# A streaming encoder step: where the turning of results stands among TensorE's products, and what the S5 kernel products wait for

## The chip, the cores and the metric

The kernel runs on one core of one Trainium2 chip. The metric is the device time of one launch in microseconds, the median of several runs. The engines of the core are called TensorE (PE in the rows, PEld its weight loads), VectorE (DVE), ScalarE (ACT), GpSimd (POOL) and SyncE (SP); each works through its own instructions in program order, and they are tied together by semaphores.

## What is computed

One inference step of a hybrid layer on 2048 prompt tokens and 8 x 16 sample tokens, model width 1024. The input is normed and multiplied by one wide matrix, and its columns are parted among three mixers:

```python
h = rms_norm(x, norm_g)
fq, fk, fv, fg, ff, su, sg, mq, mg = split_columns(h @ w_in)
fq = rms_norm(fq.reshape(B, T, N_FOX_HEADS, HEAD_DIM), fox_q_norm)
fk = rms_norm(fk.reshape(B, T, N_FOX_HEADS, HEAD_DIM), fox_k_norm)
...
fox_out = fox_attend(fq, fk, fv, logf).reshape(B, T, FOX_WIDTH) * jax.nn.silu(fg)
ssm_y, h_re, h_im = s5_mixer(su, h0_re, h0_im, a_re, a_im, log_dt, b_re, b_im, c_re, c_im, d, w_glu, b_glu)
ssm_out = ssm_y * jax.nn.silu(sg)
...
mix = jnp.concatenate([fox_out, ssm_out, mem_out], axis=-1) @ w_out
```

The change touches the first part alone, the projection `h @ w_in`, with what is computed of the S5 mixer (a diagonal state space of 16 groups) in between.

## The kernel before, in words

**Passes and visits.** The projection goes in seven passes over column groups: state (the forget logits, su and sg), keys, values, queries, memkv, memq, gate. Each pass visits 17 tiles of 128 tokens (memkv only the 2 tiles of the memory), 104 visits in all; visits 0 to 16 are the state pass, 17 to 33 the keys. A visit's product comes in three parts (`product`, L927 in the rows). The matrices are kept as a high and a low half, and the product is high x high, high x low and low x high: in parts 0 and 1 each x chunk's high half meets both halves of the weights, in part 2 the low halves of x meet the high weights. The first and the last visit of a pass go chunk by chunk instead, 3, 3 and 2 chunks to a part.

**The order.** `projection_order` writes one list of steps, and each engine's program walks through that same list and does its share of every step. After `product v, part` stand, in this order, loads of x for later visits, turnings of the input (`x`, state pass only), the next pass's weights in a pass's last visit, `first` (after part 0) and `second` (after part 1) for visit v-1, `split` (high and low halves of the next x, other passes), `turn` (after part 1, for visit v-2), and one slot of the work that is interleaved (the S5 steps, the decay, the sample's attention).

**Steps that matter here.**
- `x j`: TensorE turns input tile j (eight transposes, L882) into two banks; ScalarE first squares the input for the norm (L1193), then copies each bank twice, as high half xh (L1206) and as a whole xu (L1207); VectorE subtracts for the low half xl (L1515). Before `product v+1, 0` of the state pass comes `x` for visit v+1, placed after part 0 of visit v. In visits 7 and 12 the next item is a tile of the memory: it gets no product and only the copies xu, and the input of the next visit is then turned after part 1.
- `first v-1`, state pass: ScalarE takes the tanh of the gate (L1242, into th), VectorE scales su into `parts` (L1545), makes the logits (L1547), z (L1549), and the gate's half of `parts` (L1552).
- `turn v-2`: TensorE transposes the results of visit v-2 (L949; four of them, two for memkv and memq): `parts` in the state pass, which ScalarE copies in three instructions (L1263 twice, L1265); the normed heads, `stage`, in keys, queries, memkv and memq, of which ScalarE copies the high half (L1260) and VectorE subtracts the low half (L1595), and which SyncE then stores (L744). values and gate turn nothing.
- The banks of the state pass go in two pairs by the visit's parity, so product v+1 waits until th, su, logits and z of visit v-1 are read out.
- `s5_kern g`, g 0 to 7, in the keys pass: the pair g of the S5 kernel's impulse responses, kernels 2g and 2g+1, in three banks in rotation (kernel n in bank n mod 3), L993. Before pair g, TensorE waits until all 2g earlier kernels are copied (`s_kread`); VectorE copies each in `s5_kern_read` (L1603), one slot later, and waits for both products of the pair. Further S5 products are the drive products (L1008, read by L1615), which need the block matrix that SyncE's DMAs write, and the GLU products (L1054, followed by ScalarE's tanh L1295) in the queries pass.

## Time and profile before

| | us |
|---|---|
| median of 3 runs | 1411.63 |
| lowest, highest | 1405.93, 1411.88 |
| profiled execution, its own time | 1408.32 |
| its span, first to last instruction | 1406.4 |
| TensorE busy | 1369.0 |
| VectorE, ScalarE, GpSimd busy | 922.0, 636.6, 575.6 |

The mean granted clock of TensorE was 0.997 of full speed. The profile lists the busy time of each engine, the waits and what ended them, and the instructions in order of time. An engine's idle time counts only if the work that sets the end has to wait for it. A matmul's row runs from its start to a modelled end, so that rows of successive matmuls overlap; the distance between starts is what they cost.

### The profile page before, as it was taken

Reading aid. Unit: us, or ns where it says so; the run is one execution under the profiler, and the core shown is the slowest. Engines: PE = TensorE matmul, PEld = TensorE weight load, DVE = VectorE, ACT = ScalarE, POOL = GpSimd, SP = SyncE. Lnnn points to the kernel's source line nnn. Section 1 sums busy time; section 2 is a strip of 40 time slices with the busy share of each in tenths; the row PEclk is TensorE's granted clock in tenths of the full one; section 3 lists DMA queues with packets and bytes.
Section 4 is the critical chain, followed back from the end, with each engine's and each line's share of the span. In section 5 each row is a group of like instructions: output and inputs, shape, how many; then the busy total and the mean of one; then the engine's idle time right before and its main releaser. Section 6 shows DMA issues by size and latency. Waiting matters only on the chain.

```text
span 1406.4 us, 25060 instructions
## 1 busy us (share of the span) xinstructions
PE 1369.0 (97%) x8382; PEld 1086.1 (77%) x8382; DVE 922.0 (66%) x2025; ACT 636.6 (45%) x1364; POOL 575.6 (41%) x606
## 2 busy tenths in 40 slices
PE   8999999999999999999999999999999999999998
PEld 7999767788877777777777777777777777778886
DVE  3789755593376778666433676776776776497775
ACT  6766423332353354445333455555555655422121
POOL 2122442200033234221100556877977867644452
PEclk9999999999999999999999999999999999999999
DMA  7885699987349769787998767448458355556552
GB/s 234 295 281 199 201 268 252 275 273 228 113 139 272 248 223 266 243 266 237 313 321 264 170 189 158 107 98 181 103 109 181 83 114 196 160 169 199 191 177 89
DMA packets 211023, 284.21 MB, mean 202 GB/s; under 512 B 49809, under 2 KB 146481, under 8 KB 207409
## 3 DMA queue, kind: packets, MB, share of 16 engines
q1 hardware_dynamic: 209856, 282.61, 68.7%
q8 instruction: 69, 1.13, 0.3%
q14 instruction: 58, 0.47, 0.1%
q10 hardware_dynamic: 1040, 0.00, 0.0%
HBM read 191.12 MB, written 90.19 MB: 200 GB/s over the span
## 4 chain that ended last, share of the span: by engine, by line
PE 60%; DVE 3%; POOL 2%; ACT 2%; issue 2%; DMA 2%; SPq 1%; DVEq 0%; ACTq 0%; POOLq 0%
PE in_g L927 14%; PE attn_pv L2531 10%; PE attn_s L2601 6%; PE attn_s L2500 6%; PE attn_s L2505 5%; PE attn_pv L2601 5%; PE attn_s L2485 5%; PE attn_s L2513 2%; PE in_b L1102 1%; POOL in_hv L1810 1%; PE in_b L1054 1%; PE attn_s L2554 1%; PE attn_s L2502 1%; PE in_b L1157 1%; PE in_b L1122 1%
## 5 line engine op out<-in xcount | busy, mean ns | idle before, releaser
L927 PE MATMUL in_g<-in_wh,in_xh 128*128 128x512 f32 (+2 forms) x904 | 331.4, 380 | 6.2 <-ACT in_xh L1219 2.4
L927 PE MATMUL in_g<-in_wl,in_xh 128*128 128x512 f32 (+2 forms) x904 | 321.9, 369 | 0.0
L2807 POOL TENSOR_TENSOR attn_probs<-attn_probs,attn_probs_turned 128x512 f32<-128x512 f32 (+3 forms) x200 | 214.3, 1072 | 64.9 <-ACT attn_probs_turned L2633 40.9
L927 PE MATMUL in_g<-in_wh,in_xl 128*128 128x512 f32 (+2 forms) x904 | 236.4, 380 | 1.4 <-DVE in_xl L1532 1.3
L2847 DVE TENSOR_REDUCE attn_tops<-attn_s 128x1 f32<-128x512 f32 (+3 forms) x288 | 159.1, 596 | 108.6 <-PE attn_s L2485 108.6
L2633 ACT ACTIVATE attn_probs_turned<-attn_s 128x512 f32<-128x512 f32 (+1 forms) x352 | 161.2, 545 | 125.7 <-PE attn_s L2505 124.8
L927 PEld LDWEIGHTS in_g<-in_wh,in_xh 128*128 128x128 f32 x904 | 165.5, 189 | 40.8 <-issue 7.4
L927 PEld LDWEIGHTS in_g<-in_wl,in_xh 128*128 128x128 f32 x904 | 165.6, 189 | 27.9
L927 PEld LDWEIGHTS in_g<-in_wh,in_xl 128*128 128x128 f32 x904 | 159.1, 190 | 34.9 <-issue 5.3
L1808 POOL TENSOR_SCALAR in_hs<-in_hs 128x8 f32<-128x8 f32 (+1 forms) x53 | 19.5, 368 | 401.8 <-DVE in_hs L1559 401.8
L2531 PE MATMUL attn_pv<-attn_probs_turned,attn_v 128*64 128x256 f32 (+1 forms) x1216 | 142.1, 363 | 0.0
L1219 ACT ACTIVATE in_xh<-in_xu 128x512 fp32r<-128x512 f32 x174 | 99.6, 623 | 55.6 <-DMA in_xu<-scratch_xt 50.4
L2531 PEld LDWEIGHTS attn_pv<-attn_probs_turned,attn_v 128*64 128x64 f32 x1216 | 84.7, 136 | 41.2 <-issue 7.5
L1532 DVE TENSOR_TENSOR in_xl<-in_xu,in_xh 128x512 fp32r<-128x512 f32 x106 | 68.6, 688 | 35.7 <-ACT in_xh L1219 35.1
L1810 POOL TENSOR_TENSOR in_hv<-in_hs,all_neghalf 128x8 f32<-128x8 f32 (+1 forms) x53 | 85.4, 1611 | 4.4
L1260 ACT ACTIVATE in_x_turned<-in_tr 128x512 fp32r<-128x512 f32 (+1 forms) x53 | 27.6, 520 | 87.2 <-PE in_tr L949 78.9
L2805 POOL TENSOR_TENSOR attn_probs<-attn_probs_turned 128x512 f32<-128x512 f32 x40 | 52.7, 1327 | 30.4 <-ACT attn_probs_turned L2633 30.4
L2505 PE MATMUL attn_s<-all_x,all_y 100*128 100x512 f32 (+3 forms) x160 | 61.2, 382 | 1.6 <-ACT all_x L2622 1.6
L2500 PE MATMUL attn_s<-attn_qa,attn_ka 128*128 128x512 f32 (+3 forms) x160 | 62.1, 388 | 0.0
L2500 PE MATMUL attn_s<-all_x,all_y 128*128 128x512 f32 (+3 forms) x160 | 62.0, 388 | 0.0
L2505 PE MATMUL attn_s<-attn_qb,attn_kb 100*128 100x512 f32 (+3 forms) x160 | 61.2, 383 | 0.0
L1579 DVE TENSOR_TENSOR in_work<-in_g,in_hr 128x512 f32<-128x512 f32 (+1 forms) x53 | 31.4, 593 | 38.3 <-POOL in_hr L1813 37.2
(377 smaller groups left out, 2685.8 us busy)
## 6 DMA issues: line engine op xcount, KB each, us to landing
in_xu<-scratch_xt SPq DMA_DIRECT2D x87, 512.0 KB, 5.4
in_xl<-scratch_xt SPq DMA_DIRECT2D x34, 512.0 KB, 4.6
in_raw<-in_w_in SPq DMA_DIRECT2D x40, 256.0 KB, 5.2
scratch_xt<-in_xu SPq DMA_DIRECT2D x19, 512.0 KB, 4.4
scratch_xt<-in_xl SPq DMA_DIRECT2D x17, 512.0 KB, 5.0
scratch_k<-in_x_turned SPq DMA_DIRECT2D x17, 512.0 KB, 7.2
scratch_q<-in_x_turned SPq DMA_DIRECT2D x17, 512.0 KB, 5.4
in_x_turned<-in_x_prompt SPq DMA_DIRECT2D x16, 512.0 KB, 4.8
```

The lines of the kernel that those rows point to most:

```text
L927: last = X.matmul(g_ps[b][:, 0:m], x, ws[:, c, w0:w0 + m], start=(c == 0 and h == 0 and ws is wh), stop=(c == KC - 1 and h == 1))
L1219: F(xh[:, item_visit[j] % 2, 4 * h:4 * h + 4, :], xu[:, j % 2, 4 * h:4 * h + 4, :], ACT.Copy)\
L1532: V.tensor_tensor(xl[:, v % 3, 4 * h:4 * h + 4, :], xu[:, j % 2, 4 * h:4 * h + 4, :], fl(xh[:, v % 2, 4 * h:4 * h + 4, :]), ALU.subtract). ...
L1810: G.tensor_tensor(hv[:, 0:m], hs[:, 0:m], K.neghalf[:, 0:m], ALU.pow).then_inc(s_hchain, 1)
L2485: last = X.matmul(bank[:, at:at + n, :], qb[h][0:LANE, q], kb[h][0:LANE, keys], start=True, stop=True)
L2500: X.matmul(bank[:, part:, :], y2[h][:, keys], x2[h][:, q], start=True, stop=False)
L2505: X.matmul(bank[:, part:, :], y1[h][0:FULL, keys], x1[h][0:FULL, q], start=False, stop=True)\
L2531: last = X.matmul(v_ps[u.n % 2][lane * HD:(lane + 1) * HD, tiles[0] // 2:EACH // 2, :], vals[:, k, :], pt[:, s % SLOTS, tiles[0]::2, :], s ...
L2601: last = X.matmul(y_ps[at], ms[left][:, c, :], ws, start=(begins and c == 0 and k == 0), stop=(ends and c == HALF - 1 and k == 2))
L2633: F(pt[:, s % SLOTS, at:, :], ring_ps[ring.at["scores", s]][:, at:, :], ACT.Exp).then_inc(s_exp, 1)
L2807: E.tensor_tensor(acc[:, part:, :], acc[:, part:, :], mine, ALU.add).then_inc(added[engine], 1)
L2847: done = V.tensor_reduce(top_parts[:, d, i, 1 + k // 4:2 + k // 4], bank[:, 0:whole, :].rearrange("p n k -> p (n k)"), AX.X, ALU.max)
```

## The change

Two things are changed.

First, the place of `turn v-2`. In the state pass it stands after part 0 of visit v, ahead of the input's turning; in all other passes it stands after part 2, where it was after part 1. It is one step of the common list, so TensorE's transposes, ScalarE's copies, VectorE's low half and SyncE's store all move with it, each past what stands in between in its own program.

Second, the waits of the S5 kernel products. Kernel n, from 3 on, waits until kernel n-3, the last user of its bank, is copied, instead of each pair waiting for all before it; and VectorE's copy of kernel g waits for the products g+1 instead of for the whole pair.

```diff
--- before.py
+++ after.py
@@ -164,6 +164,8 @@
             if part == 1 and j + 3 < len(items):
                 order.append(("turned_in", j + 3))
             if p == "state":
+                if part == 0 and v >= 2:
+                    order.append(("turn", v - 2))
                 if part == 0 and items[j + 1][0] == p:
                     order.append(("x", j + 1))
                 if part == 1 and not items[j + 1][2]:
@@ -179,7 +181,7 @@
                 order.append((("first", "second")[part], v - 1))
             if part == 0 and j + 1 < len(items) and items[j + 1][0] != "state":
                 order.append(("split", j + 1))
-            if part == 1 and v >= 2:
+            if part == 2 and v >= 2 and p != "state":
                 order.append(("turn", v - 2))
             order += beside.get((v, part), [])
             if not last:
@@ -984,11 +986,12 @@
                         pe.wait_ge(s_bc, 1)
                         pe.wait_ge(s_mats, PAIRS)
                         pe.wait_ge(s_h0, 1)
-                    if g >= 1:
-                        pe.wait_ge(s_kread, 2 * g)
 
                     for c in (RE, IM):
                         for r in range(2):
+                            if c == RE and 2 * g + r >= 3:
+
+                                pe.wait_ge(s_kread, 2 * g + r - 2)
                             rows_g = slice(r * STATE, (r + 1) * STATE)
                             last = X.matmul(b_ps[(2 * g + r) % 3][0:CH, 0:L * CH], bbar[rows_g, c, g, :],
                                             ca[rows_g, c, g, 0:L, :].rearrange("p t q -> p (t q)"),
@@ -1599,7 +1602,7 @@
                     next(prepared)
                 if what == "s5_kern_read":
                     g = n[0]
-                    dve.wait_ge(s_kern, 2 * (g // 2) + 2)
+                    dve.wait_ge(s_kern, g + 1)
                     V.tensor_copy(kern[:, g, :], b_ps[g % 3][0:CH, 0:L * CH]).then_inc(s_kread, 1)
                 if what == "s5_skip":
                     dve.wait_ge(s_load, 16 * NLOAD)
```

Lines of the changed kernel are 2 or 3 higher than the same lines before (L927 is L929, L949 is L951, L993 is L996, L1549 is L1552).

TensorE, state pass, one of the middle visits; the first column is the row's number in the program, `in_parts` the results that are turned, `in_x_turned` the input. Before:

```order
434 L927 MATMUL in_g<-in_wl,in_xh 128x256
435 L882 MATMUL in_b<-all_ident,in_x_turned 128x128 [waits in_x_whole,in_x0]
436 L882 MATMUL in_b<-all_ident,in_x_turned 128x128 x7
437 L927 MATMUL in_g<-in_wh,in_xh 128x264 [waits in_x_hi]
...
452 L927 MATMUL in_g<-in_wl,in_xh 128x256
453 L949 MATMUL in_tr<-all_ident,in_parts 128x128 [waits in_turned_read,in_state_staged,in_su]
454 L949 MATMUL in_tr<-all_ident,in_parts 128x128 x3
455 L927 MATMUL in_g<-in_wh,in_xl 128x264 [waits in_x_lo]
```

After:

```order
434 L929 MATMUL in_g<-in_wl,in_xh 128x256
435 L951 MATMUL in_tr<-all_ident,in_parts 128x128 [waits in_turned_read,in_state_staged,in_su]
436 L951 MATMUL in_tr<-all_ident,in_parts 128x128 x3
437 L884 MATMUL in_b<-all_ident,in_x_turned 128x128 [waits in_x_whole,in_x0]
438 L884 MATMUL in_b<-all_ident,in_x_turned 128x128 x7
439 L929 MATMUL in_g<-in_wh,in_xh 128x264 [waits in_x_hi]
...
454 L929 MATMUL in_g<-in_wl,in_xh 128x256
455 L929 MATMUL in_g<-in_wh,in_xl 128x264 [waits in_x_lo]
```

The turn moved from the end of part 1 to the end of part 0, directly ahead of the input's transposes.

ScalarE, state pass, visits 1 and 2: tanh (`in_th`), square (`in_work,in_ssq`), the four copies of the input, and the copies of the turned results (`s_room<-in_tr`), which wait for TensorE's turn (`in_turned`). Before:

```order
26 L1242 ACTIVATE in_th<-in_g,in_half 128x256 [waits in_state_staged,in_gate_staged,in_rstd,in_products]
27 L1193 ACTIVATE in_work,in_ssq<-in_x_turned 128x1024 [waits in_ssq,in_x1]
28 L1206 ACTIVATE in_xh<-in_b 128x512 [waits in_x_lo,in_x_turned,in_xst1,in_products]
29 L1207 ACTIVATE in_xu<-in_b 128x512
30 L1206 ACTIVATE in_xh<-in_b 128x512 [waits in_x_turned]
31 L1207 ACTIVATE in_xu<-in_b 128x512
32 L1242 ACTIVATE in_th<-in_b,in_half 128x256 [waits in_state_staged,in_gate_staged,in_rstd,in_products]
33 L1263 ACTIVATE s_room<-in_tr 128x8x16 [waits in_turned]
34 L1263 ACTIVATE s_room<-in_tr 128x8x16
35 L1265 ACTIVATE s_room<-in_tr 128x2x16x8
36 L1193 ACTIVATE in_work,in_ssq<-in_x_turned 128x1024 [waits in_ssq,in_x0]
```

After:

```order
26 L1245 ACTIVATE in_th<-in_g,in_half 128x256 [waits in_state_staged,in_gate_staged,in_rstd,in_products]
27 L1266 ACTIVATE s_room<-in_tr 128x8x16 [waits in_turned]
28 L1266 ACTIVATE s_room<-in_tr 128x8x16
29 L1268 ACTIVATE s_room<-in_tr 128x2x16x8
30 L1196 ACTIVATE in_work,in_ssq<-in_x_turned 128x1024 [waits in_ssq,in_x1]
31 L1209 ACTIVATE in_xh<-in_b 128x512 [waits in_x_lo,in_x_turned,in_xst1,in_products]
32 L1210 ACTIVATE in_xu<-in_b 128x512
33 L1209 ACTIVATE in_xh<-in_b 128x512 [waits in_x_turned]
34 L1210 ACTIVATE in_xu<-in_b 128x512
35 L1245 ACTIVATE in_th<-in_b,in_half 128x256 [waits in_state_staged,in_gate_staged,in_rstd,in_products]
36 L1266 ACTIVATE s_room<-in_tr 128x8x16 [waits in_turned]
```

The first turn's three copies moved from behind the tanh of visit 2's step to ahead of its square, nine rows forward or a round of the loop less one tanh; every later turn is moved alike.

VectorE, keys pass, visits 25 and 26: the copies of kernel products (`s_room<-in_b`), the sum of squares of the heads, the low half of x, the norming in two steps, and the turn's low half (`in_x_turned<-in_tr,in_x_turned`), which waits for ScalarE's copy (`in_hi`). Before:

```order
L1603 COPY s_room<-in_b 16x256 [waits in_s5kern] x2
L1559 TENSOR_REDUCE in_hs<-in_work 128x8 [waits in_squares,in_head_rstd,in_rstd,in_products]
L1532 TENSOR_TENSOR in_xl<-in_xu,in_xh 128x512 [waits in_split_hi,in_products]
...
L1579 TENSOR_TENSOR in_work<-in_g,in_hr 128x512 [waits in_turned,in_stored1,in_head_rstd]
L1582 TENSOR_TENSOR in_stage<-in_work,in_hgain_keys 128x512 [waits in_qn]
L1595 TENSOR_TENSOR in_x_turned<-in_tr,in_x_turned 128x512 [waits in_hi]
L1603 COPY s_room<-in_b 16x256 [waits in_s5kern] x2
L1559 TENSOR_REDUCE in_hs<-in_work 128x8 [waits in_squares,in_head_rstd,in_rstd,in_products]
```

After:

```order
L1606 COPY s_room<-in_b 16x256 [waits in_s5kern] x2
L1562 TENSOR_REDUCE in_hs<-in_work 128x8 [waits in_squares,in_head_rstd,in_rstd,in_products]
L1535 TENSOR_TENSOR in_xl<-in_xu,in_xh 128x512 [waits in_split_hi,in_products]
...
L1582 TENSOR_TENSOR in_work<-in_g,in_hr 128x512 [waits in_turned,in_stored1,in_head_rstd]
L1585 TENSOR_TENSOR in_stage<-in_work,in_hgain_keys 128x512 [waits in_qn]
L1606 COPY s_room<-in_b 16x256 [waits in_s5kern] x2
L1598 TENSOR_TENSOR in_x_turned<-in_tr,in_x_turned 128x512 [waits in_hi]
L1562 TENSOR_REDUCE in_hs<-in_work 128x8 [waits in_squares,in_head_rstd,in_rstd,in_products]
```

Where a pair's copies stood behind the turn's low half they now stand ahead of it.

## Rows read from the trace of the kernel before

**Rows 1.** Page, part 1: busy time, share of the span, instructions.

```profile
PE 1369.0 (97%) x8382; PEld 1086.1 (77%) x8382; DVE 922.0 (66%) x2025; ACT 636.6 (45%) x1364; POOL 575.6 (41%) x606
```

**Rows 2.** Windows of the state and keys passes: length, each engine's busy time, PEclk, DMA share.

```profile
23.00:127.00 104.00, 103.88 (x883) 103.67 (x882) 77.95 (x217) 67.43 (x154) 23.41 (x48) 1.00 0.77 268
145.00:275.00 130.00, 123.27 (x673) 92.89 (x673) 77.64 (x129) 47.33 (x82) 46.46 (x55) 0.97 0.94 252
```

**Rows 3.** Table of waits, TensorE: us in total, times, longest us.

```profile
PE in_b L993 <- DVE s_room L1603: 3.8, 3, 1.8
PE in_tr L949 <- DVE in_stage L1582: 3.5, 7, 0.9
...
PE in_b L1008 <- DVE s_room L1615: 2.4, 1, 2.4
...
PE in_b L1054 <- ACT s_room L1295: 1.9, 4, 0.9
...
PE in_g L927 <- DVE in_z L1549: 0.4, 1, 0.4
```

**Rows 4.** Timeline, TensorE, visit 11: start us, us, engine, line, out<-in.

```profile
91.20 1.03 PE L882 MATMUL in_b<-all_ident,in_x_turned 128*128 128x128 f32 x8
...
94.00 0.60 PE L949 MATMUL in_tr<-all_ident,in_parts 128*128 128x128 f32 x4
...
96.36 0.40 PE L927 MATMUL in_g<-in_wh,in_xh 128*128 128x264 f32 x2
...
98.28 1.03 PE L882 MATMUL in_b<-all_ident,in_x_turned 128*128 128x128 f32 x8
```

**Rows 5.** Timeline, TensorE, visit 7, with two turnings side by side.

```profile
64.83 1.04 PE L882 MATMUL in_b<-all_ident,in_x_turned 128*128 128x128 f32 x8
65.70 0.60 PE L949 MATMUL in_tr<-all_ident,in_parts 128*128 128x128 f32 x4
66.06 0.37 PE L927 MATMUL in_g<-in_wh,in_xl 128*128 128x264 f32 x1
```

**Rows 6.** Timeline, ScalarE, visit 11.

```profile
91.92 0.60 ACT L1206 ACTIVATE in_xh<-in_b 128x512 fp32r<-128x512 f32 x1 [2.46 <-PE in_b L882]
...
93.85 0.50 ACT L1242 ACTIVATE in_th<-in_g,in_half 128x256 f32<-128x256 f32 x1
94.63 0.45 ACT L1263 ACTIVATE s_room<-in_tr 128x128 f32<-128x128 f32 x2 [0.29 <-PE in_tr L949]
...
95.36 1.09 ACT L1193 ACTIVATE in_work<-in_x_turned 128x1024 f32<-128x1024 f32 x1
96.33 0.20 ACT L1193 ACTIVATION_READ_ACCUMULATOR in_work<-in_x_turned 128x1 f32 x1
```

**Rows 7.** Timeline, VectorE, visit 11: z.

```profile
95.22 0.47 DVE L1549 TENSOR_SCALAR in_z<-in_g,in_half 128x256 f32<-128x256 f32 x1
```

**Rows 8.** Timeline, visit 5: ScalarE, TensorE and VectorE.

```profile
49.90 1.28 ACT L1242 ACT_TABLE_LOAD   x1
...
52.25 0.60 PE L956 MATMUL in_tr<-all_ident,s_room 128*128 128x128 f32 x4
...
52.39 0.47 DVE L1549 TENSOR_SCALAR in_z<-in_g,in_half 128x256 f32<-128x256 f32 x1
...
52.97 0.48 PE L927 MATMUL in_g<-in_wh,in_xh 128*128 128x264 f32 x2
```

**Rows 9.** Timeline, keys pass: VectorE's copy of a drive product, and TensorE.

```profile
251.66 0.44 DVE L1615 COPY s_room<-in_b 128x272 f32<-128x272 f32 x1 [4.78 <-DMA s_room<-s_room]
...
252.15 2.08 PE L1008 MATMUL in_b<-s_room 128*64 128x136 f32 x16 [2.42 <-DVE s_room L1615]
254.16 3.78 PE L927 MATMUL in_g<-in_wh,in_xl 128*128 128x512 f32 x8
```

**Rows 10.** Windows of 1 and 5 us in the keys pass; columns as in rows 2.

```profile
210.00:215.00 5.00, 3.20 (x20) 2.25 (x20) 2.48 (x5) 1.75 (x3) 1.16 (x2) 1.00 1.14 254
253.00:254.00 1.00, 1.00 (x12) 0.80 (x8) 0.00 (x0) 0.23 (x1) 0.94 (x1) 0.50 1.08 323
```

## Prediction

> **What bounds the kernel now.** I read the page first. TensorE is busy for 1369.0 of 1406.4 us [rows 1], so time can be lost or won only where it pauses, or where it is made to pause. The profiled execution took 1408.32 us, 1.9 more than its span; the median of the three runs is 1411.63, so the profile stands 3.3 us below the median. Sums are made against 1408.32 and then moved.
>
> Next, the stretches. In the state pass, from 23 to 127 us, TensorE is busy 103.88 of 104.00 us: there is no pause at all to remove. From 145 to 275, the keys pass, it is busy 123.27 of 130 and the DMA engines 0.94 [rows 2]. The table of waits then gives what the change aims at: 3.8 us in 3 waits of the kernel products (L993) for the copies of their results, and 3.5 us in 7 waits of the turns (L949) for the staged heads. Three more rows of it matter below: 2.4 us of a drive product, 1.9 us of the GLU products, 0.4 us for z [rows 3].
>
> **The state pass: does standing side by side save anything?** The trace has that case already. In visit 7 (and 12) a memory tile's second turning falls beside the turn: eight transposes at 64.83, four at 65.70, the next product at 66.06 [rows 5]. That is 1.23 us for twelve. In visit 11 the eight (91.20) and the four (94.00) stand apart: from one input's turning to the next it takes 98.28 - 91.20 = 7.08 us, one part takes 98.28 - 96.36 = 1.92, and three parts leave 1.32 for the twelve [rows 4]. The 0.09 between them lies in how the first product after a turning is shown, slower. I take 0; bounds -0.1 to 0 per visit.
>
> **The state pass: who reads the turn.** The turn's results are copied by ScalarE, which works in program order. Per visit it does: square of the next input, four copies of the turned input (xh, xu, xh, xu), tanh of the visit before, three copies of the turn. The sequence repeats, so after the change it reads the same round the loop, but the copies that stand ahead of a square now belong to a turn that TensorE issues only after part 0 of the same visit, where before they belonged to the turn of the visit before, long issued. That closes a loop: part 0, turn, three copies, square, four copies, tanh, VectorE's su, logits and z, and then part 0 of the next visit, which waits for th and z of the visit before the current one, as it writes into their banks.
>
> Before, measured from the input's turning at 91.20 [rows 4]: the first xh starts at 91.92, tanh at 93.85 [rows 6], z at 95.22 and ends at 95.69 [rows 7]. The next part 0 starts at 96.36 [rows 4]. z ends 0.67 ahead, and from z's end to a product that waits for it the trace shows 0.11 (52.86 to 52.97) [rows 8]. Headroom: 0.56 us. ScalarE did the square already in the gap before, at 95.36 [rows 6].
>
> After, measured from the end of part 0, which is now the start of the turn:
> - turn starts to first copy: 0.63 (94.00 to 94.63) [rows 4, 6]
> - three copies: 0.73 (94.63 to 95.36) [rows 6]
> - square with the reading of its sum: 1.17 (95.36 to 96.33 + 0.20) [rows 6]
> - so xh starts at 2.53 instead of 0.72: a shift of 1.81.
>
> TensorE's own part of the visit is unchanged: twelve transposes and two parts, 5.16 us, until the next part 0 is due. The shift less the headroom is 1.81 - 0.56 = 1.25 us of pause per visit. It doesn't fade: every pause moves the next turn as well, and a visit grows from 7.08 to some 8.3 us. VectorE is busy 77.95 of 104 us here [rows 2], some 5.3 of 7.08 a visit, so it can follow.
>
> **How many visits.** Visits 2 to 15 turn and are followed by a state visit or by visit 16: fourteen. In visits 7 and 12 the next input is a memory tile, with two copies instead of four, and one more group of eight transposes (0.8 us) lies in between: z then ends about 5.3 us after the turn starts, due at 6.0, no pause. That leaves 12. In visit 5 a table load of 1.28 us stands ahead of tanh, and z was late already: its product starts at 52.97, where the four extra transposes at 52.25 (0.44 by the 1.32 for twelve) would let it start at 52.69, so 0.28 was lost before [rows 8]. There the chain is 6.41 + 1.28 = 7.69 (6.41 = 5.16 + 1.25), due at 5.16 + 0.44 = 5.60: a pause of 2.09, net of the 0.28 it is +1.8. Eleven others: 11 x 1.25 = 13.75. At the pass's end ScalarE begins the next weights up to 1.36 later, behind the turn's copies, and part 0 of visit 17 waits for z already by 0.4 [rows 3]; VectorE is partly the limit there, so between 0 and 1.25, taken 0.8. Sum for the state pass: +16.4; bounds 13 (each pause 1.0) to 19 (each 1.4).
>
> **The other passes: turns a third later.** The 7 waits for the staged heads, 3.5 us at most 0.9 each, end, as the turn comes about 1.9 us later [rows 3, 4]. I take a sixth of it, 0.6, to lie before the drive products, where it is worth nothing (next part); the rest gives -2.9, bounds -3.5 to 0. What is queued behind: VectorE's low half of the turn now waits until the visit has ended, plus 0.63 and a copy of 0.6, and behind it stand the reads of part 2's slot; SyncE's store of the turn comes after `second` and the weights' load, behind it the next loads of x. Their users are a visit or more away. ScalarE's copy now stands at the visit's end ahead of the GLU's tanh. Three pairs of GLU products fall on part 2: the second of a pair needs a tanh that can only end at 0.63 + 0.60 + 0.50 = 1.7 us after the turn starts (a copy of 512 columns, a tanh of 256 [rows 6]), and could start at about 0.9 (0.35 of turn, 0.5 of the first of the pair, an estimate), so 0.8 to 0.9 is lost where 0.32 was (three of the four waits of 1.9 in all) [rows 3]. +1.8, bounds 0 to 4.
>
> **The kernel products.** VectorE's pair of copies no longer stands behind a turn where it falls on part 1; where it falls on part 2 it now does, and there the wait for one bank only covers it. Of the 3.8 us [rows 3] I expect about 2.3 to go; the third wait was for VectorE held by a late load of xu. But the time isn't kept. At 249.7 a drive product waits 2.42 us for a copy that itself waited 4.78 us for a DMA, the writing of the block matrices [rows 9], in a stretch with the DMA engines at 0.94 [rows 2]. TensorE comes there earlier and waits longer. Term 0, bounds -3.8 (the DMAs move up with it) to +2 (a read behind the turn comes late).
>
> **Sum.** +16.4 - 2.9 + 1.8 + 0 = +15.3 us. From 1408.3 that is 1423.6; from the median 1411.6 it is 1426.9. I take 1425.
>
> **Rivals.**
> (a) Faster: ScalarE is not the limit after all, z keeps its headroom, and all waits named go: -3.5 - 3.8 = -7.3, which gives 1401 to 1404. For it speaks that ScalarE is busy for only 67 of the 104 us [rows 2]; against it, that this slack lies after tanh, where the new order can't use it. It decides whether the chain from turn to z is under 5.05 us; I count 6.30. 4%.
> (b) Same: the loop costs 0.5 us or less a visit (for instance because the square's sum is read while the next copy already runs), +6, less 3 to 6 of gains: 1409 to 1416. 8%.
> (c) Clock: each pause brings TensorE to its lower level. After the wait of 2.42 us the granted clock was 0.50, that is 1.2 GHz, and eight products took 3.78 us, the sixteen small ones before them 2.08 [rows 9, 10]; half of both is lost, 2.9 us. Twelve times that is +35: 1459. Against it, in the window 210 to 215, where TensorE is busy only 3.20 of 5 us, the clock stayed 1.00 [rows 10], and the new pauses are shorter. 5%. The Trainium skill, in "TensorE: Matmul & The Clock Gate", section "A second HAM failure mode: psum-queue depth-cycling", says that short idle spells between groups of matmuls, where the banks go round, can make the clock swing between its levels; by that rule this rival would be the forecast, and this trace agrees only for the longer pause.
> (d) The other passes lose more than they gain (GLU, the sample's copies at part 2): +20 in all, 1429 to 1432. 8%.
> (e) My case, 1417 to 1429: 75%.
>
> **Range and chances.** 1415 to 1431: it takes in the bounds of the loop (13 to 19), of the other passes (-5 to +4) and the 3.3 us between profile and median. A measurement of this kernel tells about 0.5%, 7 us, from no change. Faster by more than that: (a) mostly, 0.04. Within: (b), and the lower edge of (e), 0.10. Slower: 0.86.
>
> **What the profile after would show.** Right: from 23 to 140 us TensorE pauses of about 1.2 us once a visit, waited for from L1552 (z), in 12 visits and not in 7 and 12; visits of 8.3 us; ScalarE's first xh 2.5 us after the turn starts; VectorE's preparation with more room. The waits of L951 for the staged heads gone; waits of L996 under 2 us in all; the wait of the drive products as long or longer; GLU waits about 3.5 us. Wrong: no waits for z in the state pass (then (a) or (b)), a granted clock near 0.5 after these pauses (c), or a xh that starts before the square has ended. The forecast is wrong as a whole if a state visit still takes 7.1 us.

## The result, and the profile after

The changed kernel took 1428.11 us (median of 6 runs, 1422.87 to 1430.83), the kernel before 1407.02 us (6 runs, 1403.11 to 1411.88; three of them are those shown ahead of the prediction). The ratio is 1.0148, interval [1.0131, 1.0164]: slower by 1.5%, some 21 us. Run a second time, beside 22 runs of the kernel before at 1406.47, it took 1429.18: 1.0155 [1.0136, 1.0174]. The forecast of 1425 was right in its sign, its cause and its range of 1415 to 1431. The difference was undersized: my sum said +15.3, and the figure came close in part by luck. The first three runs of before have their median at 1411.63, 4.6 us above that of all six; from 1407.0 the same sum gives 1422.3, 6 us short.

The page of the kernel after, engines' busy time, answering [rows 1]: TensorE's share falls, and its busy time grows by 8 us, though its instructions are the same 8382.

```profile
span 1427.2 us, 25062 instructions
PE 1377.0 (96%) x8382; PEld 1091.5 (76%) x8382; DVE 923.3 (65%) x2025; ACT 629.8 (44%) x1364; POOL 569.6 (40%) x606
```

Windows of after, the state pass and the keys pass, with columns as in [rows 2] (length, busy time of PE, PEld, DVE, ACT, POOL, granted clock, DMA share, GB/s):

```profile
23.00:140.00 117.00, 104.79 (x868) 102.46 (x866) 74.42 (x211) 66.08 (x154) 16.61 (x48) 1.00 0.66 230
160.00:290.00 130.00, 125.03 (x685) 94.14 (x684) 79.72 (x132) 46.64 (x85) 46.56 (x55) 0.99 0.92 250
```

TensorE had no gap in the state pass before (103.88 of 104.00); now it is idle for 12.2 of 117 us there, at full clock. The keys pass is no worse than it was. The table of waits names what is late, and answers [rows 3]:

```profile
PE in_g L929 <- DVE in_z L1552: 13.8, 13, 1.8
PE in_g L929 <- ACT in_xh L1222: 6.8, 4, 2.6
...
PE in_b L1011 <- DVE s_room L1618: 2.3, 1, 2.3
PE in_b L1057 <- ACT s_room L1298: 2.0, 1, 2.0
...
PE in_b L996 <- DVE s_room L1606: 1.5, 1, 1.5
PE in_b L1105 <- DVE in_late L1729: 1.5, 1, 1.5
```

Thirteen waits for z, 13.8 us, where there was one of 0.4. The waits of the turns for the staged heads (3.5 in 7) have shrunk to one of 0.8, those of the kernel products (3.8 in 3) to one of 1.5, and the drive product waits 2.3 as before 2.4. Most of this is what the prediction's last section asked for; not so the waits of the GLU products, 2.0 us, where it asked for 3.5. Two more rows were not asked for: xh, 6.8 us in 4 (2.4 in 2 before), and L1105 behind L1729. The table leaves out every gap under 0.15 us, which matters further down.

**One visit of the state pass.** Timeline of after, TensorE, visit 11 (columns as in [rows 4]; the first and the last row start part 0 of visits 11 and 12):

```profile
99.66 0.36 PE L929 MATMUL in_g<-in_wh,in_xh 128*128 128x264 f32 x1 [0.99 <-DVE in_z L1552]
...
101.64 0.60 PE L951 MATMUL in_tr<-all_ident,in_parts 128*128 128x128 f32 x4
102.08 1.04 PE L884 MATMUL in_b<-all_ident,in_x_turned 128*128 128x128 f32 x8
102.87 0.37 PE L929 MATMUL in_g<-in_wh,in_xh 128*128 128x264 f32 x1
...
107.94 0.48 PE L929 MATMUL in_g<-in_wh,in_xh 128*128 128x264 f32 x2 [0.98 <-DVE in_z L1552]
```

And ScalarE in the same visit, answering [rows 6]:

```profile
102.28 0.45 ACT L1266 ACTIVATE s_room<-in_tr 128x128 f32<-128x128 f32 x2 [4.08 <-PE in_tr L951]
102.61 0.62 ACT L1268 ACTIVATE s_room<-in_tr 128x256 f32<-128x256 f32 x1
103.00 1.09 ACT L1196 ACTIVATE in_work<-in_x_turned 128x1024 f32<-128x1024 f32 x1
103.96 0.22 ACT L1196 ACTIVATION_READ_ACCUMULATOR in_work<-in_x_turned 128x1 f32 x1
104.04 0.62 ACT L1209 ACTIVATE in_xh<-in_b 128x512 fp32r<-128x512 f32 x1
...
105.95 0.54 ACT L1245 ACTIVATE in_th<-in_g,in_half 128x256 f32<-128x256 f32 x1
```

Read them as one loop. The turn starts at 101.64. ScalarE has waited 4.08 us for it, with the square of the next input ready to be done but behind it in its program. Copies from 102.28, square from 103.00, the first xh at 104.04, tanh at 105.95; VectorE's z starts at 107.37 (its row stands below), and part 0 of the next visit, due at 101.64 + 5.16 = 106.80, starts at 107.94. The visit is 107.94 - 99.66 = 8.28 us long, against 7.08 before. ScalarE's idle 4.08 us and TensorE's idle 0.98 are in the same visit: two engines wait for each other in turn.

```profile
107.37 0.47 DVE L1552 TENSOR_SCALAR in_z<-in_g,in_half 128x256 f32<-128x256 f32 x1
```

**Where the 21 us went.** Each number is how many microseconds later a visit's first product starts than in the profile of before that the prediction used, counted from the program's first instruction; the last line is the end of the span. "Before again" is a second profile of the same kernel before; the kernels e1 to e11 are explained with the experiments. Visits 17, 34, 51, 68, 70 and 87 open the keys, values, queries, memkv, memq and gate passes.

```
visit   before   after   after    e1      e10     e11     e9      e2
        again            again
         (e7)             (e8)
    2   -0.25   -0.20    0.58    0.24   -0.21   -0.51   -0.06    0.05
   17   -0.25   16.45   17.28   16.94   -0.21    0.33   -0.07    0.05
   33   -2.58   14.58   15.25   16.52   -1.69   -2.19   -2.53   -1.48
   53   -2.57   14.55   15.23   16.68   -1.69   -2.22   -2.56   -1.51
   55   -2.58   12.60   13.27   16.68   -1.70   -4.17   -4.51   -3.46
   66   -3.74   12.92   13.22   14.98   -2.79   -2.97   -4.69   -1.27
   69   -3.76   13.21   13.52   14.97   -2.81   -2.67   -3.79   -0.98
   70   -3.75   15.44   15.55   14.97   -2.81   -0.68   -2.86    1.78
   75   -4.09   16.24   17.40   15.16   -3.23    1.11   -1.09    2.11
  103   -4.10   16.33   17.53   15.15   -2.71    1.25   -0.96    2.20
  end   -3.09   20.73   21.16   15.04   -1.75    5.20    3.78    5.71
```

The state pass costs 16.7 us in all three kernels that have it (16.45 + 0.20, 17.28 - 0.58, 16.94 - 0.24). The queries' turns give 1.95 back between visits 53 and 55, and most of it goes again by visit 66, where before again, free of the half clock that is told under e7, has moved from -2.58 to -3.74 and the changed kernel from 12.60 to 12.92. Then come losses that the prediction had not seen: some 2 us at visit 70, 1 to 2 before visit 75, and 4 in the attention, behind visit 103, where the second profile of before is 1 us slower than the first too.

### The profile page after: what moved, and what is told of

It reads as the page before. It is cut to its first block, busy times and chain, and to the rows that moved or that the text cites. A ratio compares the mean times of both kernels' runs of the same rounds, so it can differ in the third digit from the quotient of the medians.

```text
span 1427.2 us, 25062 instructions
## 1 busy us (share of the span) xinstructions
PE 1377.0 (96%) x8382; PEld 1091.5 (76%) x8382; DVE 923.3 (65%) x2025; ACT 629.8 (44%) x1364; POOL 569.6 (40%) x606
## 4 chain that ended last, share of the span: by engine, by line
PE 77%; DMA 5%; SPq 4%; ACT 4%; DVE 4%; issue 3%; POOL 2%; ACTq 0%; DVEq 0%; POOLq 0%
PE in_g L929 27%; PE attn_pv L2534 10%; PE attn_s L2604 6%; PE attn_s L2503 6%; PE attn_s L2508 5%; PE attn_pv L2604 5%; PE attn_s L2488 5%; DMA in_xu<-scratch_xt 2%; PE attn_s L2516 1%; PE in_b L1105 1%; PE in_tr L951 1%; SPq L721 1%; ACT in_xu L1210 1%; ACT in_xh L1209 1%; POOL in_hv L1813 1%
## 5 line engine op out<-in xcount | busy, mean ns | idle before, releaser
L929 PE MATMUL in_g<-in_wh,in_xh 128*128 128x512 f32 (+2 forms) x904 | 335.2, 384 | 23.9 <-DVE in_z L1552 13.8
L929 PE MATMUL in_g<-in_wl,in_xh 128*128 128x512 f32 (+2 forms) x904 | 322.8, 370 | 0.0
L929 PE MATMUL in_g<-in_wh,in_xl 128*128 128x512 f32 (+2 forms) x904 | 234.4, 379 | 0.4 <-DVE in_xl L1535 0.3
L929 PEld LDWEIGHTS in_g<-in_wh,in_xh 128*128 128x128 f32 x904 | 165.8, 189 | 59.2 <-issue 26.9
L929 PEld LDWEIGHTS in_g<-in_wh,in_xl 128*128 128x128 f32 x904 | 161.0, 191 | 35.4 <-issue 5.2
L929 PEld LDWEIGHTS in_g<-in_wl,in_xh 128*128 128x128 f32 x904 | 166.3, 190 | 27.0
L1598 DVE TENSOR_TENSOR in_x_turned<-in_tr,in_x_turned 128x512 fp32r<-128x512 f32 (+1 forms) x53 | 31.2, 590 | 61.0 <-ACT in_x_turned L1263 61.0
```

What stands on the lines that cost most here:

```text
L929: last = X.matmul(g_ps[b][:, 0:m], x, ws[:, c, w0:w0 + m], start=(c == 0 and h == 0 and ws is wh), stop=(c == KC - 1 and h == 1))
```

## Experiments

### e1 and e2: the two halves of the change

e1 has the new place of the turn in the state pass alone, e2 in all the other passes alone; neither has the new waits of the kernel products.

```diff
             if p == "state":
+                if part == 0 and v >= 2:
+                    order.append(("turn", v - 2))
                 if part == 0 and items[j + 1][0] == p:
                     order.append(("x", j + 1))
...
-            if part == 1 and v >= 2:
+            if part == 1 and v >= 2 and p != "state":
                 order.append(("turn", v - 2))
```

and e2:

```diff
-            if part == 1 and v >= 2:
+            if part == (1 if p == "state" else 2) and v >= 2:
                 order.append(("turn", v - 2))
```

> Only the state pass's turn is moved to part 0, ahead of the input's turning; the other passes and the kernel products' waits are as before. Theory (ScalarE's loop: turn, three copies, square, four copies, tanh, z): state visits of 8.28 us but for 7 and 12, waits for z of about 1 us in 12 visits, visit 17 begins 16.6 us later than before, and the whole is slower by 16 to 17 us, 1.2%. Rival: the changed kernel's loss of 20 us comes in good part from the other passes or from the kernel products; then this one loses 10 us or less. Second rival: the state pass's pauses also bring on spells at the lower clock in the attention, 4.3 us in the changed kernel; then this one loses about 21 us, and the spells after 780 us are here too.

> Only the turns of the other passes are moved to part 2; state pass and kernel products as before. Theory: the changed kernel's trace gave 1.9 us back in the keys pass (to which the kernel products' waits belong too), 1.95 at the first queries visits, and lost 2.2 us at visit 69 and 1.8 at visit 74, net zero: between -2 and +2 us, no difference. Rival: with the state pass undisturbed the DMAs of the keys pass meet the turns elsewhere, and it loses 4 us or more.

e1: 1423.87 us against 1407.76, ratio 1.0118 [1.01, 1.0137]. e2: 1411.08, ratio 1.0034 [1.002, 1.0047]. Together 1.0152, the whole change's 1.0148 within its interval. So the halves add up, and the state pass makes three quarters of the loss. e1 came out as expected; e2 lost 3.3 us where at most 2 were expected. e1's table of waits has the same row, and its window of the state pass the same gaps:

```profile
PE in_g L929 <- DVE in_z L1551: 13.9, 13, 1.8
```

```profile
23.00:140.00 117.00, 104.73 (x868) 102.40 (x867) 74.44 (x212) 65.91 (x154) 16.71 (x48) 1.00 0.67 230
```

### e4: the same place for TensorE, another for ScalarE

The turn stands at the end of part 0 as well, but behind the input's turning and behind `first`. TensorE's twelve transposes are side by side as in the changed kernel; ScalarE's order (square, copies, tanh, turn's copies) is that of before.

```diff
-            if part == 1 and v >= 2:
+            if part == (0 if p == "state" else 1) and v >= 2:
                 order.append(("turn", v - 2))
```

> The state pass's turn stands beside the input's turning too, but behind it and behind the step first, so that TensorE does the twelve transposes in one group while ScalarE copies the turn after its tanh, as before. All else as before. Theory: TensorE's grouping is worth nothing and the loss is ScalarE's order alone: state visits of 7.08 us, no waits for z but the one in visit 5, difference within 1.5 us of before. Rival: twelve transposes in one group disturb (banks, weight loads), and half or more of the 16 us remains. Second rival: the grouping saves 0.09 us a visit, 1.3 us in all.

1407.98 us (12 runs), ratio 1.0002 [0.9987, 1.0017]; at visit 17 it is 0.07 us behind where it was at visit 2 (0.64 against 0.57). Timeline of e4, TensorE and then ScalarE:

```profile
98.91 1.03 PE L882 MATMUL in_b<-all_ident,in_x_turned 128*128 128x128 f32 x8
99.78 0.60 PE L949 MATMUL in_tr<-all_ident,in_parts 128*128 128x128 f32 x4
```

```profile
94.47 0.50 ACT L1242 ACTIVATE in_th<-in_g,in_half 128x256 f32<-128x256 f32 x1
94.83 0.48 ACT L1263 ACTIVATE s_room<-in_tr 128x128 f32<-128x128 f32 x2
95.14 0.68 ACT L1265 ACTIVATE s_room<-in_tr 128x256 f32<-128x256 f32 x1
95.54 1.14 ACT L1193 ACTIVATE in_work<-in_x_turned 128x1024 f32<-128x1024 f32 x1
```

Two things follow. Grouping the transposes is worth nothing (my term of 0 holds). And TensorE's place for the turn is harmless: the loss is made by the place that ScalarE gets with it, since one list orders all engines.

### e5: the changed kernel with the square moved ahead

The whole change, but ScalarE does the square of the next input ahead of the turn's copies, in the time in which it waited.

```diff
+            mine = []
+            for step in order:
+                if step[0] == "x" and mine and mine[-1][0] == "turn":
+                    mine.insert(-1, ("square", step[1]))
+                mine.append(step)
...
```

> The changed kernel with one thing different: ScalarE does the square of the next input ahead of the turn's three copies (it stood behind them), everything else as changed. Theory: the loop gets shorter by the square's 1.04 us (from 1.36 to 2.40 after the turn's start), so of each pause of 1.21 us some 0.1 to 0.2 remains: state visits of 7.1 to 7.3 us, z in time or late by 0.1 to 0.2, the state pass 14 us shorter than in the changed kernel; the whole 1 to 4 us over before. Rival: the pauses come from the doubled group of transposes or from PSUM, not from ScalarE's order; then it stays at about +20 us. The tanh after a table load in visit 5 stays late by some 0.6 us.

1416.08 us (6 runs), ratio 1.0066 [1.0045, 1.0086]. The state pass now loses 3.8 us (4.20 - 0.39 at visits 17 and 2) instead of 16.7. In the timeline of e5 ScalarE goes from the copies straight to xh, 1.36 us after the turn started at 93.80, and does the square at 97.47, behind tanh:

```profile
94.44 0.45 ACT L1272 ACTIVATE s_room<-in_tr 128x128 f32<-128x128 f32 x2 [3.06 <-PE in_tr L951]
94.77 0.62 ACT L1274 ACTIVATE s_room<-in_tr 128x256 f32<-128x256 f32 x1
95.16 0.66 ACT L1215 ACTIVATE in_xh<-in_b 128x512 fp32r<-128x512 f32 x1
...
97.47 1.11 ACT L1202 ACTIVATE in_work<-in_x_turned 128x1024 f32<-128x1024 f32 x1
```

Taking 1.04 us (104.04 - 103.00) of square out of the loop takes out 12.9 us of 16.7. This is the strongest evidence for the loop: one instruction of ScalarE, moved without touching TensorE, gives back nearly all. 0.2 us a visit stays (7.29 us from turn to turn against 7.08), and it is the same loop: z ends at 99.00 in this profile, and part 0 starts at 99.10, 5.30 behind the turn and not 5.16, a gap too short for the table of waits. The whole kernel is 8.3 us over before where 1 to 4 were expected; what the state pass doesn't explain lies in the other passes and in the clock, below.

### e3: the kernel products' waits alone

The second part of the change on top of before, its diff as shown ahead of the prediction.

> Only the waits of the S5 kernel products are changed, all turns stand where they stood before. Theory (my term of 0): the waits of L993, 3.8 us in 3, shrink to 1 to 3 us, the drive product of visit 32 waits as much longer, as the DMAs of the block matrix set that moment, and visit 35 begins within 0.7 us of before; no difference, within 1.5 us. Rival: the block matrix moves up with the kernel products and 2 to 3 us are won.

1406.14 us (12 runs), before 1407.64 (27 runs), ratio 0.9995 [0.9982, 1.0008]. Its table of waits:

```profile
PE in_b L1007 <- DVE s_room L1614: 2.9, 2, 1.7
...
PE in_b L992 <- DVE s_room L1602: 2.0, 2, 1.3
```

The waits of the kernel products fell from 3.8 to 2.0. The drive products' 2.9 are no loss: the second profile of before has 2.9 in 2 as well (and 3.8 for the kernel products). Yet from visit 17 to visit 33 e3 is only 0.4 us quicker than that profile. The interval leaves the term of 0 open by some 1.8 us to either side; whether half a microsecond is won can't be told.

### e7: before again

> The kernel before once more, for its profile. Theory: the 4.3 us that the changed kernel's profile lost after 780 us, at 811 and at 1251, in spells at 1.2 GHz, are a matter of chance that meets every one of these kernels (e4_beside had them, e1_state had not): a second profile of before may have them too, at some 796 and 1236 us, or not. Rival: only kernels with moved turns have them.

One execution, 1405.31 us. Its profile serves as a second base line, and it was needed: TensorE ran at half clock in the first profile of before, behind the drive product's wait [rows 9, 10], and not in this one, in a stretch with the same instructions:

```profile
252.00:258.00 6.00, 4.70 (x34) 3.44 (x31) 4.10 (x8) 1.75 (x3) 1.84 (x2) 1.00 1.04 337
```

It gains 2.33 us by visit 33 (-0.25 to -2.58), 2.15 of them behind visit 27, where that spell lies. Its own waits for the drive products there were 1.6 and 1.3 us, where the first profile had one of 2.42. Compared with the first profile alone the changed kernel's keys pass seems to win 1.9 us; compared with the second it wins nothing, though it has a spell at half clock there of its own, 3.4 us from 268.6.

### e10 and e11: which of the other passes

e2 parted: e10 turns late in the keys pass alone, e11 in queries, memkv and memq.

```diff
-            if part == 1 and v >= 2:
+            if part == (2 if p == "keys" else 1) and v >= 2:                # e10
+            if part == (1 if p in ("state", "keys") else 2) and v >= 2:     # e11
```

> Before, with the turns after part 2 in the keys pass alone; the state pass, values, queries, memkv and memq are as before, and so are the kernel products' waits. Of the seven waits for the staged heads, those of the keys pass go; in the runs so far the turns of the other passes after part 2 gave a mean granted clock of about 0.994 against 0.997 before, some 4 us. If the keys pass brings it (the turn and its reads then crowd the stretch from 150 to 260 us, where the spells at half clock stood), its clock is about 0.995 and its time 1409 to 1411. If the queries and later passes bring it, the clock stays at 0.997 and the time is 1406 to 1408.

> Before, with the turns after part 2 in queries, memkv and memq; keys and the state pass as before. Expected by offsets: visits 53 to 55 give back about 1.9 us, visit 70 costs 2.8 and visit 75 costs 1.8 again. If these two late pauses, of ScalarE's xh and of the sample's keys, are what brings the lower clock, the mean clock is about 0.995 and the time 1410 to 1413; if the keys pass brings it, 0.997 and 1407 to 1409.

e10: 1407.96 us, ratio 1.0014 [1.0003, 1.0025], mean clock 0.9967. e11: 1410.71, ratio 1.0025 [1.0014, 1.0037], mean clock 0.9955. By the ranges set down both point to the queries and later passes as what brings the lower clock; but e10 loses a little as well, and the sum of both, 1.0039, is e2's 1.0034 within the intervals.

In e10 two of the seven waits for the staged heads went (2.9 us in 5 are left), and the kernel products' waits fell from 3.8 to 2.4, since VectorE's copies now stand ahead of the turn's low half. From visit 17 to visit 31 it is 2.0 us quicker than before again. It loses them at visit 32, ScalarE and TensorE:

```profile
243.28 1.15 ACT L1219 ACTIVATE in_xh<-in_xu 128x512 fp32r<-128x512 f32 x2 [8.59 <-DMA in_xu<-scratch_xt]
```

```profile
244.05 0.47 PE L927 MATMUL in_g<-in_wh,in_xh 128*128 128x512 f32 x1 [2.15 <-ACT in_xh L1219]
```

In before again SyncE issues that load of x at 233.94, here at 233.83, and xh starts at 242.07 there: TensorE comes sooner and the load does not. All seven profiles with late turns in the keys pass have this wait for xh, 1.0 to 2.4 us (0.2 in e6), and none of the six others has it.

### e9: why visit 70 is late

The timeline of SyncE (start, us to issue, line) of the changed kernel, in visit 68, the memkv pass's first. The store of the turn that stands in the last queries visit, 67, goes ahead of the loads of the memq pass's weights:

```profile
534.00 0.37 SPq L746 DMA_DIRECT2D scratch_q<-in_x_turned  x1
534.41 5.45 SPq L642 DMA_DIRECT2D in_raw<-in_w_in  x8
```

Visit 68's product starts at 526.84, so the store goes out 7.16 us behind it; before it was 519.23 - 513.86 = 5.37. With the turn a part later, its store is 1.8 us later, and eight weight loads wait behind it in SyncE's queue. ScalarE, which splits these weights, then waits for the DMA, and xh stands behind the splits in its program, and the product behind xh:

```profile
540.70 1.40 ACT L1189 ACTIVATE in_wh<-in_raw,in_gains 128x512 fp32r<-128x512 f32 x2 [1.22 <-DMA in_raw<-in_w_in]
...
542.72 1.14 ACT L1222 ACTIVATE in_xh<-in_xu 128x512 fp32r<-128x512 f32 x2
```

```profile
543.60 0.47 PE L929 MATMUL in_g<-in_wh,in_xh 128*128 128x512 f32 x1 [2.57 <-ACT in_xh L1222]
```

e9 is e2 with that one visit's turn back at part 1:

```diff
-            if part == (1 if p == "state" else 2) and v >= 2:
+            early = p == "state" or last and p == "queries"
+            if part == (1 if early else 2) and v >= 2:
                 order.append(("turn", v - 2))
```

> The other passes' turns at part 2 as in e2_others, but for one visit: in the last visit of the queries, 67, the turn stays after part 1. State pass and kernel products as before. Theory: in e2_others SyncE's store of that turn came 7.6 us after visit 68 began instead of 5.8, the eight loads of the memq weights stand right behind it, so ScalarE splits them late and visit 70 begins 2.8 us late. Here the store is early again: visit 70 begins no later than visit 69 did (step under 0.5 us), no spell at the lower clock there, and the whole loses 2 to 3 us less than e2_others, that is 1.5 to 3 us over before. Rival: the step at visit 70 stays, as the loads are late through full DMA queues or ScalarE is late through its own copies.

The store went out 5.75 us behind visit 68's product (515.07 - 509.32), and the step from visit 69 to 70 fell from 2.76 us in e2 to 0.93 (under 0.5 was expected); the wait for xh from 3.08 to 1.40:

```profile
525.29 0.47 PE L928 MATMUL in_g<-in_wh,in_xh 128*128 128x512 f32 x1 [1.40 <-ACT in_xh L1220]
```

So the mechanism is shown for 1.8 of the 2.8 us; what makes the rest isn't. In the time it is not to be seen, where 2 to 3 us were expected: 1412.85 us, ratio 1.0033 [1.0019, 1.0046], the same as e2. In the two profiles e9 leads e2 by 2.81 us at visit 69, by 4.64 at 70, and by 3.16 at 103: most of what visit 70 won goes again between visits 71 and 75, where e9 was at half clock and e2 was not. The windows of e9 and of e2:

```profile
539.00:541.00 2.00, 2.00 (x6) 1.61 (x6) 1.83 (x4) 0.00 (x0) 1.78 (x2) 0.50 0.91 261
```

```profile
541.00:546.00 5.00, 3.73 (x18) 3.14 (x19) 4.38 (x12) 0.74 (x4) 2.02 (x4) 1.00 0.74 164
```

### e6: the parts that promised a gain

Late turns in keys, values and queries except their last visits, the new waits of the kernel products, and everything else as before.

> State pass as before; the turns of keys, values and queries visits at part 2 except in the last visit of each of these passes; memkv and memq at part 1 as before; kernel products with the new waits. Theory: keeps what the changed kernel won (1.9 us in the keys pass, 1.95 at visits 53 and 54) and drops what it lost (2.2 us at visit 69, 1.8 at 74): the last visit of the projection 2 to 4 us earlier than before, the whole 2 to 4 us faster, 0.15 to 0.3%, if the granted clock stays as before. Rival: the waits move, and the shift of the pauses in keys and queries brings on more spells at the lower clock, as in e2_others (mean granted clock 0.9947 against 0.9970): then no gain.

1408.72 us (12 runs), ratio 1.0004 [0.9988, 1.002]. Its waits for the staged heads are down to 1.9 us and those of the kernel products to 1.4, yet nothing of that is in the time, where 2 to 4 us were expected: it came out as the rival has it, with a mean clock of 0.9953 against 0.9973. No version tried is measurably faster than the kernel before.

### e8: the changed kernel again, and the clock

> The changed kernel once more, beside the other two on one chip, for its clock and for the places of its spells at half clock: about 1428 us. The spells at the same places as in its first profile (268, 545, 811, 1252 us) would speak for a cause in the order of work there; other places for chance from run to run. Clock 0.994.

1429.18 us, as expected, mean clock 0.9952. Windows in the two profiles of the changed kernel, first the first, then the second; the column behind POOL is the granted clock:

```profile
812.00:817.00 5.00, 5.00 (x25) 4.02 (x24) 2.86 (x5) 1.78 (x6) 4.38 (x6) 0.50 1.02 240
1252.00:1255.00 3.00, 3.00 (x11) 2.61 (x11) 3.00 (x3) 0.00 (x0) 2.31 (x2) 0.50 0.00 1
```

```profile
814.00:819.00 5.00, 5.00 (x25) 3.67 (x23) 3.78 (x6) 1.12 (x4) 3.98 (x5) 0.50 0.99 213
1254.00:1256.00 2.00, 2.00 (x6) 1.52 (x5) 2.00 (x4) 0.00 (x0) 2.00 (x2) 0.50 0.00 0
```

TensorE ran at half clock in two stretches of the attention, at the same places in both, far from anything that was changed; the spells in the passes moved (268 and 545 us in the first, 263, 454 and 557 in the second). In before again, shown here, and in e3 the same stretches of the attention, 20 us earlier, are at full clock:

```profile
790.00:800.00 10.00, 9.99 (x68) 7.74 (x68) 7.35 (x16) 6.97 (x21) 9.09 (x9) 1.00 0.88 201
1230.00:1240.00 10.00, 8.58 (x37) 6.35 (x36) 9.23 (x13) 5.62 (x9) 4.28 (x4) 1.00 0.38 131
```

The table takes all kernels together (each ratio against the runs of before on the same chip): the mean granted clock over all runs of each, span times clock (an estimate of the spans at full clock throughout, which takes the time at half clock to be TensorE's alone), and the microseconds at half clock in the profiled execution, ahead of the span's last few.

```
            runs  ratio    clock    span x clock   at half clock: attention, elsewhere
before       22   1        0.9977      1401.6      0     6.8   (again: 0, 0)
e3           12   0.9995   0.9977      1401.3      0     0
e4           12   1.0002   0.9969      1402.0      10.2  3.4
e1            4   1.0118   0.9970      1417.7      0     3.4
e10          12   1.0014   0.9967      1401.6      3.4   3.4
e11          12   1.0025   0.9955      1402.3      10.2  6.8
e6           12   1.0004   0.9953      1399.7      0     6.8
e2            9   1.0034   0.9947      1402.2      10.2  6.8
e9           10   1.0033   0.9933      1400.9      10.2  10.2
e5            6   1.0066   0.9928      1404.5      10.2  6.8
after         6   1.0148   0.9938      1416.9      10.2  6.8
after again   5   1.0155   0.9952      1419.6      10.2  10.2
```

The row of before is one of three sets of its runs; the other two, of 20 runs (beside e1, e2, e4, e5) and 27 (beside e3, e6, e9), gave 0.9970 and 0.9973. Two costs come apart. The waits: e1 +16, the changed kernel +15 to +18, e2, e3, e4, e6 and e9 to e11 0 within 2 us or so, e5 +3. The clock: e1 has that of the runs of before beside it; those with late turns in the queries passes have 0.9928 to 0.9955, 0.0020 to 0.0042 under before's beside them, which is 3 to 6 us of 1405 by this estimate. e4, whose median is before's, has the attention's stretches at half clock in its profiled execution too, which took 1412.6 us. So they are no property of one order; that an order makes them more or less frequent is what the mean clocks suggest. Which of the moved steps does it isn't shown. Before visits 70 and 75 there are new pauses, and a stretch at half clock begins 1.5 us behind the start of visit 70 in the first profile of the changed kernel and 13 us behind it in e5, e9, e11 and the second; but e9, which has the smaller pause there, has no better clock.

## Why the prediction came out as it did

**What bounds the kernel.** Right: TensorE's path alone counts, the state pass had no gap, and each pause put there went into the time.

**Standing side by side.** Taken as 0. The twelve cost 102.87 - 101.64 = 1.23 us, the very figure of [rows 5], and e4 shows that this is no gain.

**The loop.** Right in each step. From the turn's start: xh at 2.40 (I had 2.53, since the next copy starts before the reading of the sum has ended, as 96.33 and its 0.20 in [rows 6] could have told), z's end at 6.20, part 0 at 6.30. By my sum part 0 comes at 6.41. The pause is 6.30 - 5.16 = 1.14, and part 0 behind a pause takes 1.98 (101.64 - 99.66) instead of 1.92: 1.20 a visit for the 1.25 of the forecast.

**How many visits.** Eleven others at 1.2 (the offsets grow by 1.15 to 1.23 a visit): 13.1, forecast 13.75. Visit 5: +1.77 (1.8 forecast), where the table load sits in the loop. The pass's end: +0.76 (0.8). What failed is "z then ends about 5.3 us after the turn starts, due at 6.0, no pause": visits 7 and 12 lost 0.5 each. z was in time, but I had asked for z alone. Timeline of after, visit 7, TensorE and ScalarE:

```profile
68.81 1.04 PE L884 MATMUL in_b<-all_ident,in_x_turned 128*128 128x128 f32 x8
72.02 1.06 PE L884 MATMUL in_b<-all_ident,in_x_turned 128*128 128x128 f32 x8 [0.26 <-ACT in_xu L1210]
```

```profile
70.78 1.10 ACT L1210 ACTIVATE in_xu<-in_b 128x512 f32<-128x512 f32 x2
```

The second turning of the visit needs the two banks that xu reads, and xu stands behind the copies and the square too. In all the state pass gave 16.7 for 16.4: two errors, of +1.0 and -0.7, that nearly cancel.

**The turns a third later.** Forecast -2.9. In the queries it came, -1.95 (visits 53 to 55). In the keys pass e10 wins 2.0 us up to visit 31 and loses them at visit 32, to the wait for xh; I had let a gain turn into a wait for a DMA only at the drive products. The queries' gain goes the same way: the changed kernel waits for xh 2.2 us at visit 59 and 0.9 at visit 61, before again 1.2 once. The named cost, "behind it the next loads of x. Their users are a visit or more away", is the step that failed, twice. These loads do come too late for a TensorE that is ahead, though that the store ahead of them delays them isn't shown. And I looked at them alone, not at the eight loads of the memq weights, which stand behind part 0 of the memkv pass's first visit, next to the turn that now stands in the visit before. That cost 2 us at visit 70. VectorE's program did the same to the sample's keys: the copies L1728 and L1729 stand behind a turn's low half that now comes a part later (17.3 us later than in the profile of before, while visit 74, in which it falls, starts 14.4 later), and TensorE waits. Timeline of after, VectorE and TensorE:

```profile
573.01 0.42 DVE L1598 TENSOR_TENSOR in_x_turned<-in_tr,in_x_turned 128x256 fp32r<-128x256 f32 x1 [2.06 <-ACT in_x_turned L1263]
...
575.10 0.67 DVE L1729 COPY in_late<-in_b 128x512 f32<-128x512 f32 x1
```

```profile
575.91 0.63 PE L1105 MATMUL in_b<-all_ident,in_late 128*128 128x128 f32 x4 [1.48 <-DVE in_late L1729]
```

**The GLU products.** Forecast +1.8 from three waits of 0.8 to 0.9. In the first such pair of after, in visit 62, the tanh ends when I said, 485.26 + 0.48 = 485.74, 1.6 us after the turn starts at 484.13, and the pair's second product waits for it and starts at 485.79. But the first product of the pair takes 0.92 us (four matmuls 0.23 apart) and not my 0.5, so only 0.3 is lost a pair, no more than before, in a gap too short for the table. The one long wait, 2.0 in visit 62, was 0.9 before, and one of 0.9 for a DMA is gone. In sum the stretch from visit 61 to 66 takes 1.0 us less than in before again, where the forecast had 1.8 more.

**The kernel products.** Forecast 0; e3 gives 0.9995 [0.9982, 1.0008].

**The rivals.** (a) and (b) fall with e1: z is late, 12 visits of 1.2. (c) falls where I had placed it: after twelve pauses of 1 us the granted clock of the state pass is 1.00, in the changed kernel and in e1. The Trainium skill's rule in "TensorE: Matmul & The Clock Gate", section "A second HAM failure mode: psum-queue depth-cycling", didn't hold for pauses of this size. But I had asked about the clock in the state pass alone, and had no term at all for the clock elsewhere, which by the table's estimate costs the changed kernel 3.5 to 5.5 us without a wait to show for it. (d), the other passes losing more than they gain, is in part what happened: 1428 lies at the upper end of my case, 1 us under (d)'s 1429 to 1432, and e2's +0.34%, 4.8 us, is (d) on its own, where I had the other passes at -1.1 us. So the state pass was right step by step, and the rest was wrong in sign.

## What to carry to other kernels

Where one list of steps orders all engines, a step that is moved for one engine is moved for each: follow it on every engine, and ask there what was done in idle time before it and now stands behind it (the square), and in each DMA queue what stands behind its store (the weights). If moving a step closes a loop through an in-order engine, its cost is the loop's length less TensorE's own work, every round; moving the one ready instruction out of the loop (e5) gave back 12.9 of 16.7 us. And when waits that went don't show in the time, look for the next wait for a DMA behind them, as at visit 32 of e10, and compare the mean granted clock over all runs, not one profile.

## What was new about the hardware

TensorE's lower clock did not come where TensorE paused most. Twelve pauses of 1 us, 8.3 us apart, left the clock at 1.00. The same two stretches of the attention, the first with TensorE busy for all of its 5 us, were granted 0.50 in seven profiles and 1.00 in five (in e10 one was and one wasn't), though the kernels differ only in what ran more than 100 us earlier. One profile of a kernel can thus differ from the next by where the clock was low: the two profiles of before differ by 3.1 us in span, 2.2 of them between visits 27 and 33, where one ran at half clock for 6.8 us and the other not at all.
